# A decoder layer in float32: weight sums of the 7-product pieces of the down projection made by adding DMAs into a DRAM scratch, four pairs of k tiles per half instead of three

## Chip, cores and metric

One NeuronCore of a Trainium2 chip. The metric is the device time of one execution in microseconds (us), as the median of several. Engines are named as in the profile: PE (TensorE), DVE (VectorE), ACT (ScalarE), POOL (GpSimd), SP (SyncE, which here only issues DMAs).

## What is computed

A decoder layer on 256 tokens of width 2048. The change touches its last part, the feed-forward network:

```python
h = rmsnorm(x, g_pre_ffn[l])
up = causal_dwconv(h @ w_up[l], w_fconv[l], b_fconv[l])
gate, val = jnp.split(up, 2, axis=-1)
x = x + rmsnorm((jax.nn.gelu(gate, approximate=True) * val) @ w_down[l], g_post_ffn[l])
```

`w_up` is 2048 x 11264, `w_down` 5632 x 2048. Ahead of it stand, in this order, the input projections with latent attention (16 heads), the gates and the attention's output projection, a gated linear recurrence, the output projection, and a cross-attention; their result, the residual x3, goes into this part and is added at its end.

## The kernel before

**Pieces.** All weights stream through four slots of `raw` (128 partitions x 2048 columns, 1 MB a slot). Each piece is split into a high part (ACT, a rounding copy to float32r, `hi`, L1151) and a low part (DVE, raw minus high, `lo`, L1686), both in the same slot of `wsp`. PE multiplies with three terms: high x high, low x high, high x low (`TERMS`, `rows_mm`, L607; for whole feature tiles L544, where the first two are one matmul). SP issues the load of a piece when the low part of the piece four before it is done; ACT starts on a piece when PE has left the piece four before it; ACT and DVE run two pieces ahead of PE (`LEAD`). Each engine runs its instructions in the order of the code; ACT and DVE also evict tiles, and what is queued behind a waiting instruction waits too. Semaphores `landed`, `hi_done`, `lo_done` and `gemm_step` count these steps.

**The feed-forward stages.** The hidden features are made in three groups, of 16, 16 and 12 tiles of 128 (`GROUPS`). For each group 8 (or 6) up rounds (`up_round`) of four pieces make two hidden tiles each: ACT and DVE evict, scale, add the convolution and apply the gelu; POOL multiplies gate and value (L2550). Then the down stage multiplies the group's hidden tiles (the k tiles) with `w_down` and adds the result to the output.

**Seven products.** In the first two groups the down stage has two halves of 1024 output columns, 12 pieces each (`DN_PLAN`, `dn_half`). A pair of k tiles, the two blocks of 128 tokens and the two blocks of 512 columns make a 2 x 2 block product. A "plain" piece does it with 8 block products, 24 matmuls of 512 columns. Three of eight pairs do it in seven products (Strassen's scheme in Winograd's form). Such a pair has two pieces: "first" (9 matmuls), with weight blocks as they are, and "made" (12 matmuls), with sums and differences of weight blocks. DVE makes those sums from the "first" piece in the slot behind it (`sums_two`, `sums_rest`, L2303, L2309, L2310), so a "made" piece has no load. The last pair is two "single" pieces (12 matmuls each). The left-hand sums, the forms, come from two hidden tiles: POOL makes them (`form_sums`), ACT the high part (`form_high`, L1541), DVE the low part (`form_low`, L2218), in the up rounds.

**Where forms and x3 lie.** `forms` is laid over `big_a`, in which x3 stays for the residual. So x3 is stored in a DRAM tensor (`x3_kept`, in the trace `x_kept`) by a DMA of ACT behind up round 0 (L1585), and loaded back before the last group. ACT waits for the store behind its round 1:

```python
up_round(1)
if n == 0:
    act.wait_ge(x3_spilled, 16)
with act.Fori(1, up.trips // 2) as r:
    up_round(r * 2, formed=r - 1)
    up_round(r * 2 + 1)
```

**Between halves.** The product sums take four banks of PSUM, which the next half's plain pieces need. When the last "made" piece of a half is done ACT copies one bank (`q1_keep`, L1617) and DVE combines the others (`products_out`, L2332 to L2343); `plain_out` adds the plain banks.

**POOL** normalizes in attention (L2496), does elementwise work of the recurrence (L2509 to L2523) and of the up rounds, and issues no DMA.

## Time and profile before

| | us |
|---|---|
| median of 3 runs | 1728.7 (1728.68 to 1729.89) |
| the profiled execution | 1728.19 |
| its span | 1726.4 |
| PE busy | 1717.3 (99%) |
| DVE busy | 1210.6 (70%) |
| ACT busy | 943.0 (55%) |
| POOL busy | 168.9 (10%) |

The span runs from the first to the last instruction of the profiled execution. PE busy is the time in which a matmul was in flight. MB is 1024 x 1024 bytes where a transfer's size is told (the profile gives KB), and GB/s is the profile's own. The mean DMA rate over the span is 194 GB/s.

### The profile page before, as it was taken

The page shows a single profiled execution, that of the slowest core. Times are in us where ns is not written, and L with a number is a line of the kernel's source. Part 1 is how long each engine was busy: PE and PEld are TensorE (multiplying, and loading weights), DVE is VectorE, ACT ScalarE, POOL GpSimd, SP SyncE. Part 2 cuts the span into 40 slices and gives each one's busy share as a digit, 9 for nine tenths or more (in the row PEclk, how much of TensorE's full clock was granted, in tenths as well). Part 3 has the DMA queues.
Part 4 walks back from the last instruction along what each step waited for, and adds up shares of the span by engine and source line. Part 5 has one row for each costly group of instructions (what it writes and reads, how often), then busy time and mean ns, then how long its engine had stood idle before and what let it go on. Part 6 is the DMA issues. An engine that isn't in the chain of part 4 may idle for free.

```text
span 1726.4 us, 25016 instructions
## 1 busy us (share of the span) xinstructions
PE 1717.3 (99%) x8932; PEld 1463.5 (85%) x8932; DVE 1210.6 (70%) x1519; ACT 943.0 (55%) x1201; POOL 168.9 (10%) x201
## 2 busy tenths in 40 slices
PE   9999999999999999999999999999999999999998
PEld 8888888888888888888888888888888888888886
DVE  7766665467788874446567687778877778877766
ACT  7656655443667763334447565555555555445553
POOL 0012210000344520000000001110001110000000
PEclk9999999999999999999999999999999999999999
DMA  9644456565556565556655465554665554585552
GB/s 341 201 136 157 152 198 230 191 244 187 174 177 190 173 230 191 192 193 233 219 178 173 146 214 181 189 194 162 209 214 183 179 177 162 207 271 184 194 215 102
DMA packets 218719, 334.31 MB, mean 194 GB/s; under 512 B 5792, under 2 KB 162080, under 8 KB 215072
## 3 DMA queue, kind: packets, MB, share of 16 engines
q1 hardware_dynamic: 212736, 318.53, 55.1%
q10 hardware_dynamic: 5920, 14.94, 2.4%
q8 instruction: 40, 0.66, 0.2%
q14 instruction: 23, 0.19, 0.0%
HBM read 329.25 MB, written 4.19 MB: 193 GB/s over the span
## 4 chain that ended last, share of the span: by engine, by line
PE 98%; DVE 1%; DMA 0%; ACT 0%; issue 0%; DVEq 0%; SPq 0%
PE ps L544 51%; PE ps L607 36%; PE ps L1023 3%; PE ps L560 3%; PE ps L819 1%; PE ps L747 1%; PE ps L669 1%; PE ps L658 0%; PE ps L639 0%; PE ps L776 0%; PE ps L752 0%; PE ps L769 0%; DVE wsp L1686 0%; PE ps L663 0%; PE ps L777 0%; PE ps L907 0%
## 5 line engine op out<-in xcount | busy, mean ns | idle before, releaser
L1686 DVE TENSOR_TENSOR wsp<-raw,wsp 128x2048 fp32r<-128x2048 f32 (+3 forms) x307 | 673.1, 2209 | 256.5 <-ACT wsp L1151 249.6
L1151 ACT ACTIVATE wsp<-raw 128x2048 fp32r<-128x2048 f32 (+3 forms) x296 | 537.3, 1831 | 197.5 <-PE ps L607 182.9
L544 PE MATMUL ps<-asp,wsp 128*128 128x512 f32 x3064 | 542.4, 339 | 0.4 <-DVE wsp L1686 0.2
L544 PEld LDWEIGHTS ps<-asp,wsp 128*128 128x128 f32 x3064 | 469.6, 188 | 71.1 <-issue 1.4
L607 PE MATMUL ps<-wsp,hsp 128*128 128x512 f32 x2004 | 459.2, 390 | 0.2 <-DVE wsp L1686 0.2
L607 PEld LDWEIGHTS ps<-wsp,hsp 128*128 128x128 f32 x2004 | 375.7, 188 | 78.8 <-DVE wsp L1686 1.1
L544 PE MATMUL ps<-hsp,wsp 128*128 128x512 f32 (+1 forms) x1936 | 349.7, 340 | 0.0
L544 PEld LDWEIGHTS ps<-hsp,wsp 128*128 128x128 f32 x1936 | 297.5, 188 | 42.9
L607 PE MATMUL ps<-wsp,asp 128*128 128x512 f32 x768 | 175.6, 389 | 0.0
L1162 ACT ACTIVATE cr<-ps 128x256 f32<-128x256 f32 x185 | 69.3, 380 | 191.0 <-PE ps L544 171.9
L607 PEld LDWEIGHTS ps<-wsp,asp 128*128 128x128 f32 x768 | 143.9, 188 | 29.8
L2550 POOL TENSOR_TENSOR scr<-scr 128x256 f32<-128x256 f32 x44 | 34.2, 797 | 984.3 <-DVE scr L2246 984.3
L1551 ACT ACTIVATE scr<-scr,par 128x256 f32<-128x256 f32 x88 | 48.2, 596 | 63.4 <-DVE scr L2235 63.4
L2240 DVE SCALAR_TENSOR_TENSOR scr<-scr,par 128x255 f32<-128x255 f32 x88 | 42.5, 484 | 25.5 <-ACT scr L1551 25.2
L1694 DVE TENSOR_TENSOR cr<-ps,cr 128x256 f32<-128x256 f32 x88 | 35.1, 420 | 34.1 <-ACT cr L1162 34.1
L2518 POOL TENSOR_TENSOR scr<-scr 128x256 f32<-128x256 f32 x16 | 28.6, 1789 | 246.7 <-ACT scr L1342 246.7
L1579 ACT ACTIVATE hsp<-scr 128x256 f32 (+1 forms) x44 | 18.5, 420 | 53.1 <-POOL scr L2550 53.1
L560 PE MATMUL ps<-wsp,asp 128*128 128x512 f32 (+1 forms) x256 | 47.5, 341 | 0.0
L560 PEld LDWEIGHTS ps<-wsp,asp 128*128 128x128 f32 x256 | 40.0, 188 | 5.8
L2280 DVE TENSOR_TENSOR hsp<-scr,hsp 128x256 f32 (+1 forms) x44 | 19.8, 450 | 35.4 <-ACT hsp L1579 35.4
L1602 ACT ACTIVATE wsp<-raw 128x2048 fp32r<-128x2048 f32 x12 | 23.1, 1922 | 36.8 <-DVE raw L2310 25.0
L1261 ACT ACTIVATE scr<-scr,st 128x128 f32<-128x128 f32 (+1 forms) x32 | 14.4, 450 | 48.2 <-DVE st L1868 48.2
(291 smaller groups left out, 1191.8 us busy)
## 6 DMA issues: line engine op xcount, KB each, us to landing
raw<-in_w_up SPq DMA_DIRECT2D x88, 1024.0 KB, 5.3
raw<-in_w_in SPq DMA_DIRECT2D x64, 1024.0 KB, 5.4
raw<-in_w_down SPq DMA_DIRECT2D x40, 1024.0 KB, 5.0
raw<-in_w_in SPq DMA_DIRECT2D x32, 768.0 KB, 4.5
raw<-in_w_o_mla SPq DMA_DIRECT2D x16, 1024.0 KB, 5.2
raw<-in_w_o_lru SPq DMA_DIRECT2D x16, 1024.0 KB, 5.1
raw<-in_w_out SPq DMA_DIRECT2D x16, 1024.0 KB, 4.9
raw<-in_w_ukv SPq DMA_DIRECT2D x8, 1024.0 KB, 5.5
```

Of the source, the lines that this page charges most:

```text
L544: mm = pe.matmul(ps[:, bank, 0:w], lhs(part, k), x[:, 0:w], start=(f and part == 0), stop=(l and n == 1))
L560: mm = pe.matmul(o, x, r, start=(f and part == 0), stop=(l and n == 1))
L607: mm = pe.matmul(ps[:, bank, :], src[:, k, low * T + m * P:low * T + (m + 1) * P], wsp[:, c, part, cols], start=(first and t == 0), stop=( ...
L1023: mm = pe.matmul(ps[:, bank, :], lhs(low), wsp[:, slot, part, quarter(block)], start=(first and t == 0), stop=(last and t == 2))
L1151: act.activation(wsp[:, p0 % SLOTS, 0, 0:n], raw[:, p0 % SLOTS, 0:n], ACT.Copy).then_inc(hi_done, 1)
L1162: act.activation(cr[:, slot, :], ps[:, bank, T:2 * T], ACT.Copy, scale=scale).then_inc(cross_done, 1)
L1551: act.activation(UC[2 * v + e], UR[2 * v + e], ACT.Identity, scale=col(W_F + 2 * P, m), bias=col(B_F, m)).then_inc(up_bias, 1)
L1686: dve.tensor_tensor(wsp[:, slot, 1, 0:n], raw[:, slot, 0:n], wsp[:, slot, 0, 0:n].bitcast(F32), ALU.subtract).then_inc(lo_done, 1)
L1694: return dve.tensor_tensor(dst, ps[:, bank, 0:T], cr[:, slot, :], ALU.add)
L2240: own.mark(dve.scalar_tensor_tensor(out=buf[:, 1:T], in0=src[:, 0:T - 1], scalar=col(W_F + P, m), in1=buf[:, 1:T], op0=ALU.mult, op1=ALU.add))
L2518: own.mark(pool.tensor_tensor(IG[e], IG[e], XC[e], ALU.mult))
L2550: pool.tensor_tensor(HID[e], UC[e], UC[2 + e], ALU.mult).then_inc(hid_out, 1)
```

## The change

**Plan.** Each half now has four product pairs (0, 2, 4, 6) and four plain ones (1, 3, 5, 7); the "single" pieces are gone. The last piece of a half is a plain pair.

**Weight sums.** For each "made" piece (8 a group) POOL builds the 128 x 2048 block in the DRAM tensor `dn_sums`: two copies of 128 x 512 from `w_down`, two DMAs that add to them, then twice a copy inside the scratch and an adding DMA. It does so for batches of 3, 3 and 2 pieces and waits after each of six steps of a batch. The first group's sums stand in POOL's order between attention and the recurrence, the second group's between the recurrence and the up rounds. SP loads a "made" piece from the scratch; a "first" piece is loaded in two DMAs, without its first block of 512 columns, which its matmuls don't use. The additions on DVE are gone.

**Forms.** Each group has four forms instead of three, written in the odd up rounds 1, 3, 5, 7 instead of 2, 4, 6. ACT's wait for the store of x3 moves in front of round 1.

**Order.** `q1_keep` and `products_out` stand one piece later in ACT's and DVE's order (behind piece 12 of a stage, where the last "made" piece is number 10; before, behind piece 11 with the last "made" piece number 9).

```diff
-DN_PLAN = [("plain", 0), ("plain", 2), ("plain", 4), ("plain", 6), ("first", 1), ("made", 1),
-           ("first", 3), ("made", 3), ("first", 5), ("made", 5), ("single", 14), ("single", 15),
...
+DN_HALF = [("plain", 1), ("plain", 3), ("first", 0), ("made", 0), ("first", 2), ("made", 2),
+           ("plain", 5), ("first", 4), ("made", 4), ("first", 6), ("made", 6), ("plain", 7)]
+DN_PLAN = DN_HALF + DN_HALF
...
+DN_SUMS = [DN_MADE[0:3], DN_MADE[3:6], DN_MADE[6:8]]
...
# SP
+                        sp.wait_ge(lo_done, dn.p(0, c) - SLOTS + 1)
+                        if kind == "first":
+                            sp.dma_start(raw[:, slot, 512:1024], w_dn[:, k, c0 + 512:c0 + 1024]).then_inc(landed[slot], 16)
+                            sp.dma_start(raw[:, slot, 1024:2048], w_dn[:, k + 1, c0:c0 + 1024]).then_inc(landed[slot], 16)
+                        else:
+                            at = DN_MADE.index(c) + len(DN_MADE) * n
+                            sp.wait_ge(dn_sums_step, sums_ready(n, c))
+                            sp.dma_start(raw[:, slot, :], dn_sums[at]).then_inc(landed[slot], 16)
...
# ACT
                     if n == 0:
                         act.wait_ge(x3_sq, 2)
                         act.dma_start(x3_kept, a_tok).then_inc(x3_spilled, 16)
-                    up_round(1)
-                    if n == 0:
                         act.wait_ge(x3_spilled, 16)
+                    up_round(1, formed=0)
                     with act.Fori(1, up.trips // 2) as r:
-                        up_round(r * 2, formed=r - 1)
-                        up_round(r * 2 + 1)
+                        up_round(r * 2)
+                        up_round(r * 2 + 1, formed=r)
...
# DVE
                     for c in range(LEAD, 24 + LEAD):
-                        if c + 1 in DN_FIRST:
-                            sums_two(c + 1)
...
-                        if c + 1 in DN_FIRST:
-                            sums_rest(c + 1)
-                        if c in (11, 23):
-                            products_out(c // 12)
+                        if c in (12, 24):
+                            products_out(c // 24)
...
# POOL
+            def weight_sums(n, cs, done):
...
+                def step(count):
+                    done[0] += 16 * count * len(cs)
+                    pool.wait_ge(dn_sums_step, done[0])
+                for at in cs:
+                    for e in range(2):
+                        pool.dma_start(to(at, e), block(at, 0, 0)).then_inc(dn_sums_step, 16)
+                step(2)
+                for at in cs:
+                    pool.dma_start(to(at, 0), block(at, 0, 1), accum_op=ALU.add).then_inc(dn_sums_step, 16)
+                    pool.dma_start(to(at, 1), block(at, 1, 0), accum_op=ALU.add).then_inc(dn_sums_step, 16)
+                step(2)
+                for frm, into, k, b in ((0, 2, 1, 0), (2, 3, 1, 1)):
+                    for at in cs:
+                        pool.dma_start(to(at, into), to(at, frm)).then_inc(dn_sums_step, 16)
+                    step(1)
+                    for at in cs:
+                        pool.dma_start(to(at, into), block(at, k, b), accum_op=ALU.add).then_inc(dn_sums_step, 16)
+                    step(1)
```

**In ACT's order**, behind up round 0 of the first group (`wsp<-raw` is the high part of a piece, `cr<-ps` an eviction, `hsp<-scr` the hidden tiles' high part, `x_kept` the store's target). Before:

```order
L1579 ACTIVATE hsp<-scr 128x256 [waits hid_out] x2
L1585 DMA x_kept<-big_a 128x4096 [waits x3_sq]
L1151 ACTIVATE wsp<-raw 128x2048 [waits landed2,gemm_step]
L1151 ACTIVATE wsp<-raw 128x2048 [waits landed3,gemm_step]
L1162 ACTIVATE cr<-ps 128x256 [waits up_ready,tile_out,gemm_step] x2
```

Now:

```order
L1590 ACTIVATE hsp<-scr 128x256 [waits hid_out] x2
L1596 DMA x_kept<-big_a 128x4096 [waits x3_sq]
L1162 ACTIVATE wsp<-raw 128x2048 [waits landed2,gemm_step,x3_spilled]
L1552 ACTIVATE forms<-scr 128x4x128 [waits fm_raw]
L1162 ACTIVATE wsp<-raw 128x2048 [waits landed3,gemm_step]
L1173 ACTIVATE cr<-ps 128x256 [waits up_ready,tile_out,gemm_step] x2
```

The wait on `x3_spilled` has come to the first high part behind the store, and a form stands between the two high parts.

**In DVE's order**, around the end of the first half of group 0 (`scr<-cols_in,ps` and the next three are `products_out`). Before:

```order
L1686 TENSOR_TENSOR wsp<-raw,wsp 128x1024 [waits hi_done] x2
L2332 TENSOR_TENSOR scr<-cols_in,ps 128x512 [waits q1_out,gemm_step]
L2340 TENSOR_TENSOR cols_in<-scr,ps 128x512 [waits dn_out]
L2341 TENSOR_TENSOR cols_in<-ps,scr 128x512
L2343 TENSOR_TENSOR cols_in<-ps,cols_in 128x512 [waits dn_out]
L1686 TENSOR_TENSOR wsp<-raw,wsp 128x2048 [waits hi_done] x2
```

Now:

```order
L2300 TENSOR_TENSOR wsp<-raw,wsp 128x1536 [waits hi_done]
L1687 TENSOR_TENSOR wsp<-raw,wsp 128x2048 [waits hi_done] x3
L2316 TENSOR_TENSOR scr<-cols_in,ps 128x512 [waits q1_out,gemm_step]
L2324 TENSOR_TENSOR cols_in<-scr,ps 128x512 [waits dn_out]
L2325 TENSOR_TENSOR cols_in<-ps,scr 128x512
L2327 TENSOR_TENSOR cols_in<-ps,cols_in 128x512 [waits dn_out]
L1687 TENSOR_TENSOR wsp<-raw,wsp 128x2048 [waits hi_done]
```

Behind the last "made" piece two low parts stand ahead of `products_out` now (pieces 11 and 12), where both of the "single" pieces stood, and one instead of two follows before the next half's first product piece.

## Rows read from the trace of the kernel before

**Rows 1.** The page: busy time of each engine, and the granted clock by slice.

```profile
span 1726.4 us, 25016 instructions
...
PE 1717.3 (99%) x8932; PEld 1463.5 (85%) x8932; DVE 1210.6 (70%) x1519; ACT 943.0 (55%) x1201; POOL 168.9 (10%) x201
...
PEclk9999999999999999999999999999999999999999
```

**Rows 2.** Waits of PE, whole span: who was waited for, us, times, longest.

```profile
PE ps L1128 <- ACT mask L1666: 2.2, 1, 2.2
...
PE ps L544 <- DVE wsp L1686: 0.2, 1, 0.2
...
PE ps L607 <- DVE wsp L1686: 0.2, 1, 0.2
```

**Rows 3.** The chain of waits: start us, us, what.

```profile
271.48 114.29 PE ps L607 x504
...
1007.33 163.20 PE ps L544 x928
...
1192.30 14.29 PE ps L1023 x63
```

**Rows 4.** The chain, at the end of group 0's first half.

```profile
1206.61 0.61 ACT cols_in L1617
...
1207.32 0.70 DVE scr L2332
...
1209.93 2.21 DVE wsp L1686
```

**Rows 5.** Timeline of DVE, down stage: start us, us, instruction, count, idle before.

```profile
1180.56 1.22 DVE L2303 TENSOR_TENSOR raw<-raw 128x1024 f32<-128x1024 f32 x1
...
1184.62 0.69 DVE L2310 TENSOR_TENSOR raw<-raw 128x512 f32<-128x512 f32 x1
```

**Rows 6.** Tile forms: ns min/median/max of one form's high part, and when.

```profile
L1541 ACT ACTIVATE forms<-scr x6: 615/616/637, 1042.5 to 1397.3; 128x512 f32 x6
```

**Rows 7.** Windows: stretch, busy of PE, PEld, DVE, ACT, POOL, clock, DMA share, GB/s.

```profile
263.00:443.00 180.00, 180.00 (x824) 150.03 (x823) 104.78 (x107) 81.80 (x65) 0.56 (x1) 1.00 0.62 212
0.00:35.00 35.00, 33.41 (x150) 27.66 (x151) 25.84 (x51) 25.71 (x40) 1.78 (x11) 1.00 0.98 348
```

**Rows 8.** Timeline of ACT around the store of x3.

```profile
1018.80 0.35 ACTq L1585 DMA_DIRECT2D x_kept<-big_a  x1
1019.25 3.73 ACT L1151 ACTIVATE wsp<-raw 128x2048 fp32r<-128x2048 f32 x2
```

**Rows 9.** DMA issues by line, whole span: KB each, us to landing.

```profile
x_kept<-big_a ACTq DMA_DIRECT2D x1, 2048.0 KB, 6.5
```

**Rows 10.** Timeline of DVE, up round 1: the low parts of its pieces.

```profile
1021.20 4.49 DVE L1686 TENSOR_TENSOR wsp<-raw,wsp 128x2048 fp32r<-128x2048 f32 x2 [1.53 <-ACT wsp L1151]
```

**Rows 11.** End of the span: timeline of PE, then windows as in rows 7.

```profile
1721.32 0.67 PE L1128 MATMUL ps<-scr,mask 128*128 128x256 f32 x2 [2.19 <-ACT mask L1666]
...
1719.00:1721.00 2.00, 0.13 (x1) 0.00 (x0) 1.57 (x8) 1.03 (x4) 0.00 (x0) 1.00 0.00 0
...
1723.00:1724.00 1.00, 0.00 (x0) 0.00 (x0) 0.25 (x1) 0.00 (x0) 0.00 (x0) 0.67 1.03 354
1724.00:1725.00 1.00, 0.00 (x0) 0.00 (x0) 0.00 (x0) 0.00 (x0) 0.00 (x0) 0.50 1.05 366
```

**Rows 12.** Timeline of POOL: end of attention, the recurrence, the first up round.

```profile
443.05 0.74 POOL L2518 TENSOR_TENSOR scr<-scr 128x256 f32<-128x256 f32 x1 [179.48 <-ACT scr L1342]
446.76 0.74 POOL L2521 TENSOR_TENSOR scr<-scr 128x256 f32<-128x256 f32 x1 [2.98 <-ACT scr L1349]
...
1017.21 1.55 POOL L2550 TENSOR_TENSOR scr<-scr 128x256 f32<-128x256 f32 x2 [390.11 <-DVE scr L2246]
```

**Rows 13.** DMA issues by line: the weights of this stage and the output.

```profile
raw<-in_w_o_mla SPq DMA_DIRECT2D x16, 1024.0 KB, 5.2
...
out<-raw SPq DMA_DIRECT2D x7, 256.0 KB, 2.5
```

More of the change, by code:

```diff
@@ L77, with sums_ready, __init__ @@
 W_F, B_F = 256, 640
+DN_SUMS = [DN_MADE[0:3], DN_MADE[3:6], DN_MADE[6:8]]
+def sums_ready(n, c):
+    turn = [c in cs for cs in DN_SUMS].index(True)
+    return 16 * 8 * (n * len(DN_MADE) + sum(len(cs) for cs in DN_SUMS[:turn + 1]))
 class Phase:
-    def __init__(self, after, trips, ends, crosses=True, made=()):
+    def __init__(self, after, trips, ends, crosses=True, twice=()):
         self.trips, self.ends, self.n = trips, ends, len(ends)
@@ L101, in __init__ @@
         self.x_end = self.x0 + (self.tiles * trips if crosses else 0)
-        self.made = (after.made if after else []) + [self.p0 + c for c in made]
-        assert self.n % SLOTS == 0 and (not made or trips == 1)
+        self.twice = (after.twice if after else []) + [self.p0 + c for c in twice]
+        assert self.n % SLOTS == 0 and (not twice or trips == 1)
     def p(self, i, c):
@@ L118, in landed @@
         at = self.p0 + c
-        skipped = sum(q < at and q % SLOTS == at % SLOTS for q in self.made)
-        return i * (16 * self.n // SLOTS) + 16 * (at // SLOTS + 1 - skipped)
+        more = sum(q <= at and q % SLOTS == at % SLOTS for q in self.twice)
+        return i * (16 * self.n // SLOTS) + 16 * (at // SLOTS + 1 + more)
 class Tally:
@@ L161 @@
     if _count % 16 == 0:
-        PH_DN.append(Phase(PH_UP[-1], 1, [0] * 24, made=DN_MADE))
+        PH_DN.append(Phase(PH_UP[-1], 1, [0] * 24, twice=DN_FIRST))
     else:
@@ L357, in piece_size @@
         def piece_size(ph, i, c):
-            if ph.n == len(DN_PLAN) and c < ph.n and DN_PLAN[c][0] == "single":
-                return 1024
             if ph is PH_A:
@@ L1043, in dn_half @@
                         (kind, pair), slot = DN_PLAN[c], c % SLOTS
-                        k0, k1 = (pair, pair) if kind == "single" else (2 * pair, 2 * pair + 1)
+                        k0, k1 = 2 * pair, 2 * pair + 1
                         arrive(dn, 0, c)
@@ L1060, in dn_half @@
                                         mm = x_mm(c, k, m, b, first=(k == k0))
+                        elif c == mine[-1]:
+                            for m in range(2):
+                                for b in range(2):
+                                    for k in (k0, k1):
+                                        mm = x_mm(c, k, m, b, last=(k == k1))
+                                    if (m, b) != (1, 1):
+                                        mm.then_inc(dn_done, 1)
                         elif kind == "plain":
@@ L2500, in _, with to, block @@
                 attention(u)
+            def weight_sums(n, cs, done):
+                def to(at, first, count=1):
+                    return dn_sums[len(DN_MADE) * n + DN_MADE.index(at)][:, first * 512:(first + count) * 512]
+                def block(at, k, b):
+                    k, c0 = GROUPS[n][0] + 2 * DN_PLAN[at][1] + k, (at // 12) * 1024 + b * 512
+                    return w_dn[:, k, c0:c0 + 512]
+                def step(count):
[16 more added lines that the diff above has]
+                    step(1)
+            sums_done = [0]
+            for cs in DN_SUMS:
+                weight_sums(0, cs, sums_done)
             n0 = own.n
@@ L2552, in up_pair @@
                 def up_pair(r):
-                    own.n, own.off = n0 + 6 * n, r * 2
+                    own.n, own.off = n0 + 8 * n, r * 2
                     up_round(r * 2)
+                    form_sums(n, r)
                     up_round(r * 2 + 1)
-                    form_sums(n, r)
                 if fn == 16:
                     up_pair(0)
-                    with pool.Fori(1, up.trips // 2 - 1) as r:
+                    with pool.Fori(1, up.trips // 2) as r:
                         up_pair(r)
-                    for i in range(up.trips - 2, up.trips):
-                        up_round(i)
                 else:
```

73 lines of the change are left out of this document (23 added, 50 removed).

## Prediction

> **What bounds the kernel now.** I read the page first: TensorE (PE) is busy for 1717.3 of 1726.4 us at full granted clock [rows 1]. Then the waits of PE: the longest is 2.2 us, at the end, and only two of 0.2 us are for work that the change touches [rows 2]. So the time is the number of matmuls times their pace, and a change gains only by removing matmuls; every microsecond in which PE must wait is added. The chain of waits says the same and gives the pace: 504 matmuls of 512 columns take 114.29 us, 63 in the product pieces 14.29 us, 0.2268 us each [rows 3]. VectorE (DVE) and ScalarE (ACT) are under 75% busy [rows 1], so relief for them is worth nothing by itself.
>
> **The matmuls.** A pair of k tiles costs 24 matmuls as a plain piece (2 k, 2 row blocks, 2 column blocks, 3 terms) and 21 as products (9 in a "first" piece, 12 in a "made" one). A half had 3 pairs as products and 5 plain (the last cut into two "single" pieces): 63 + 120 = 183. It now has 4 and 4: 84 + 96 = 180. Three matmuls fewer in each of 4 halves (2 groups of 16 tiles, 2 halves): 12 x 0.2268 = **2.7 us less**, all on the bounding engine.
>
> **The hand-over between halves.** Before, the plain pieces of half 1 (and the first up piece behind half 1) waited a little for a DVE subtraction of 2.21 us that stood behind the four additions of the product sums [rows 4]: two waits of PE of 0.2 us [rows 2]. Now that subtraction stands ahead of these additions. Its input needs PE to be through with piece 8, and 9 + 12 matmuls (4.8 us) follow before the last "made" piece ends, so it is done by then; the additions take 0.61 + 4 x 0.7 = 3.3 us beside a plain piece of 5.4 us. Worth **0.4 us less**.
>
> **Additions taken off DVE.** Of each "made" piece 1.22 + 0.69 + 0.69 us of DVE work go [rows 5], 12 times, 31 us. PE waited for none of it [rows 2], so this counts nothing. The added fourth form per group costs ACT 0.62 us [rows 6], and DVE about as much for 512 columns [rows 5], between pieces as the other three; nothing.
>
> **The loads of the down stage.** "made" pieces had no load; now each has one of 1 MB, and "first" has 0.75 MB instead of 1. A half needs 4 x 1 + 4 x 1.75 = 11 MB in 180 x 0.2268 = 40.8 us. Full DMA share moved about 348 GB/s [rows 7], 3.0 us per MB, so 33 of 40.8 us. A buffer is free when its subtraction is done, which is more than a piece ahead of its use; following pieces one by one with 2 us from issue to the first byte and 3.1 us per MB, the tightest piece lands 5.6 us before it is needed. No term, but little is left for anything slower.
>
> **The spill of x3, moved wait.** This is the term that decides. Forms lie over the buffer that holds x3, so x3 must be stored in DRAM before the first form is written. The first form is now made in up round 1, not round 2, so ACT's wait for the store has moved from behind round 1 to directly behind its issue. ACT issued the store at 1018.80 [rows 8]; it needs 6.5 us to landing [rows 9], so ACT stands until 1025.3. What is queued behind it is the high part of round 1's third piece, which began at 1019.25 [rows 8]. Its low part on DVE began 1.95 us after that and takes 2.25 us (4.49 for two) [rows 10]: now ready at 1025.3 + 1.95 + 2.25 = 1029.5. PE wants the piece three pieces after 1007.33; 928 matmuls (29 pieces) take 163.20 us, 5.63 a piece [rows 3], so at 1024.2. Before, it was ready at 1023.45, only 0.8 us early. So PE stands still for **5.3 us**, once. The form (0.62 us on ACT) goes between this piece and the next, which is then ready near 1032.4 against 1035.1 wanted, and the pieces of round 2 some 1.5 us early: no second stall. Nothing gives this back, since PE never waits there otherwise. In the second group the wait doesn't exist.
>
> **The clock behind that stall.** No row has a gap of 5 us inside the work. At the end PE was idle for 2.19 us before 1721.32 at granted clock 1.00; after its last matmul, which ended at 1721.99, the clock was 0.67 in 1723 to 1724 and 0.50 from 1724 on [rows 11], that is half speed within 2 us of idleness. A stall of 5.3 us may well end at 1.2 GHz. What half speed then costs is between nothing (it comes back at once) and a piece's 5.6 us (one piece at half speed); no row shows a return, so I take the middle, **2.8 us more**. The Trainium skill (TensorE: Matmul & The Clock Gate, Part 1) says that the throttled clock is the default and only activity releases it, which speaks against this change: a stall is paid a second time after it ends. By it the sum has this term, by the 2.2 us gap that passed at full clock it has not; the end of the trace agrees with the rule as to the fall, and no run here yet shows the return.
>
> **The sum.** 1728.2 (the profiled execution; span 1726.4 and 1.8 around it) - 2.7 - 0.4 + 5.3 + 2.8 = 1733.2; the median shown is 0.5 above the profiled one, so **1733.7 us**.
>
> **Is the scratch made in time?** GpSimd (POOL) now issues 64 DMAs of 256 KB for each group, in 18 steps with a wait after each. The first group's stand between attention's last multiply, ended 179.48 us before 443.05, at 263.6, and the first multiply of the recurrence at 443.05; the next really waited-for one is at 446.76 [rows 12], so there are 183 us. No row has a DMA issued by POOL, a DRAM to DRAM copy or an add. Nearest rows: 2 MB in 6.5 us [rows 9] and 256 KB in 2.5 us [rows 13], so 1.9 us fixed and 2.3 us per MB. With an add counted as twice its bytes, a batch of 3 takes 5.4 + 8.8 + 3.6 + 5.4 + 3.6 + 5.4 = 32 us, that of 2 takes 25: **90 us alone**, 35 of them fixed and 55 transfer. Beside it the weight loads have a DMA share of 0.62 [rows 7]. If both queues take turns the transfers double: 145 us. If the loads go first, 55 / 0.38 + 35 = 180 us. I take 145, since two queues with work are likelier to alternate; cost nothing, cover 38 us. The second group has the 390 us before 1017.21 [rows 12]. The weight loads themselves may be slowed by this: a load is issued when the piece in its buffer is split, some 4 us after PE gave back the buffers that this split writes, and it is wanted when they come free again, four pieces of 5.4 us later. So it may take some 17 us, against 5.2 now [rows 13].
>
> **Rivals.**
> 1. *The clock stays up.* As above without the 2.8: 1731.0 us, a loss of 0.13% that a measurement can't tell. For it: the 2.2 us gap. Against: the fall within 2 us at the end [rows 11]. 15%.
> 2. *The scratch is late.* POOL's queue is in order, so attention's successor, the recurrence, waits behind the DMAs; its scan on DVE and with it the splitting of weights wait, and PE within some 5 us. It decides if an add costs more than three times a plain transfer: with four, (18 + 73) x 2 + 35 = 217 us, 34 us late, 1768 us. Making descriptors on POOL could do the same. For it: a chain of 18 waits, and a window that fits by 38 us only by assumption. Against: nearest rows give 90 to 180. 22%.
> 3. *The other side: no stall.* The stored x3 lands by 1020.0 (1024.2 less the 4.2 us of splitting), or ACT's wait isn't at the queue's head. Then only the saved matmuls show: 1725.6 us, 0.18% less, not slower. It decides at a landing of 1.2 us, which a 2 MB store can't reach at any rate in the rows; left is that I misread who needs the piece. 8%.
> 4. *Loads starve* in the down stage or beside the adds, by some pieces of a few us: about 1738. 5%.
>
> **How the numbers follow.** A measurement of this kernel tells 0.2%, 3.5 us, from no change. My forecast, stall and clock, has 50%; its own range is 1731 to 1736.6 (clock cost 0 to 5.6), nearly all of it slower by over 0.2%: 0.43. With rivals 2 and 4 slower is 0.69. Same: 0.07 of the forecast, rival 1, most of rival 3, 0.28. Faster 0.03. The range starts at 1730, leaving out rival 3, and ends at 1757, leaving out the worse half of rival 2.
>
> **What would show it.** PE's matmul count 8920 instead of 8932; one wait of PE of about 5 us near 1024, on DVE's low part behind ACT, with ACT idle until the store lands; granted clock under 1.00 right after; no PE wait near the halves; POOL's last DMA of the first group landed before the recurrence's multiply. Wrong would be a recurrence that starts late, PE waits on loads, or no gap near the first up rounds.

## The result, and the profile after

| | before | after |
|---|---|---|
| median | 1728.7 | 1799.29 (1798.07 to 1806.63, 5 runs) |
| the profiled execution | 1728.19 | 1806.63 |
| its span | 1726.4 | 1804.5 |

The changed kernel takes 1.0422 times as long (95% interval 1.0405 to 1.0439). The forecast was 1733.7 with a range up to 1757. Two of the five executions took 1806.4 and 1806.6 us, three 1798.1 to 1799.3; the trace is of one of the longer, and no trace shows where the others are 7 us shorter. The page of the changed kernel, busy times and granted clock:

```profile
span 1804.5 us, 25148 instructions
PE 1718.7 (95%) x8920; PEld 1465.3 (81%) x8920; DVE 1191.2 (66%) x1485; ACT 950.1 (53%) x1203; POOL 259.2 (14%) x335
...
PEclk9999999999659999999999999999999999999999
```

Beside [rows 1]: PE's busy time is the same within 1.4 us, the matmuls are 12 fewer, and the span is 78 us longer. So the time is in waits. PE's waits, in the same view as [rows 2]:

```profile
PE ps L554 <- DVE wsp L1687: 76.8, 2, 71.5
PE ps L1139 <- ACT mask L1667: 2.2, 1, 2.2
...
PE ps L665 <- ACT wsp L1199: 0.6, 1, 0.6
```

The first line holds two waits: 76.8 - 71.5 = 5.3 us is the stall behind the store of x3, to the tenth what the prediction's steps give. The other, 71.5 us, was rival 2's. The 0.6 us lie 10 us into the kernel; the trace of the kernel before has no such wait there, and of the experiments' traces, in which that part of the code is the same, some have it and some have not. PE's timeline has both stalls (start us, us, instruction, count, idle before):

```profile
532.09 7.58 PE L554 MATMUL ps<-hsp,wsp 128*128 128x512 f32 x32 [71.49 <-DVE wsp L1687]
...
1103.72 8.63 PE L554 MATMUL ps<-asp,wsp 128*128 128x512 f32 x33 [5.30 <-DVE wsp L1687]
```

At the first, the profile names DVE's low part as what PE waited for. Following the waits back one engine at a time: DVE's low part stands in its order behind the recurrence's scan, the scan waits for POOL's multiply, and POOL was not computing at all. The waits of DVE and of ACT over the whole span, of each the longest line on POOL:

```profile
DVE scr L1980 <- POOL scr L2533: 82.5, 9, 73.4
...
ACT asp L1335 <- POOL scr L2519: 74.8, 4, 68.3
```

The timeline of POOL, from attention's last multiply to the first one of the recurrence:

```profile
264.32 3.36 POOL L2496 DMA_DIRECT2D dn_sums<-in_w_down  x6
277.29 0.90 POOL L2499 DMA_DIRECT2D dn_sums<-in_w_down  x1 [9.60 <-DMA dn_sums<-in_w_down]
287.57 0.83 POOL L2500 DMA_DIRECT2D dn_sums<-in_w_down  x1 [9.38 <-issue]
...
298.32 0.81 POOL L2500 DMA_DIRECT2D dn_sums<-in_w_down  x1 [9.08 <-issue]
...
471.13 0.56 POOL L2496 DMA_DIRECT2D dn_sums<-in_w_down  x1 [8.54 <-DMA dn_sums<-in_w_down]
...
518.59 0.82 POOL L2507 DMA_DIRECT2D dn_sums<-in_w_down  x1 [3.77 <-issue]
523.04 0.72 POOL L2528 TENSOR_TENSOR scr<-scr 128x256 f32<-128x256 f32 x1 [3.62 <-DMA dn_sums<-in_w_down]
```

The first group's sums take 264.3 to 523.0, 259 us, where the prediction had 145 and 183 us of room. Two kinds of waits alternate: for the landing of a step's DMAs ("<-DMA", the program's own wait), and in front of a DMA in the middle of a step ("<-issue", a wait for nothing that the profile shows). The second kind was in no step of the prediction. The recurrence started at 523.0 instead of 443 [rows 12].

The half clock behind the stalls shows in windows, columns as in [rows 7]:

```profile
534.00:536.00 2.00, 2.00 (x9) 1.74 (x8) 2.00 (x6) 0.89 (x1) 0.00 (x0) 0.55 1.05 371
536.00:538.00 2.00, 2.00 (x14) 1.72 (x13) 2.00 (x7) 0.00 (x0) 0.00 (x0) 1.00 1.09 354
...
1102.00:1103.00 1.00, 0.00 (x0) 0.00 (x0) 1.00 (x1) 1.00 (x1) 0.00 (x0) 0.71 0.00 0
1103.00:1105.00 2.00, 1.28 (x4) 1.10 (x5) 2.00 (x3) 1.12 (x3) 0.00 (x0) 0.50 0.07 13
1105.00:1107.00 2.00, 2.00 (x8) 1.71 (x7) 2.00 (x4) 0.00 (x0) 0.00 (x0) 0.50 0.94 308
1107.00:1109.00 2.00, 2.00 (x9) 1.71 (x7) 1.66 (x6) 1.58 (x3) 0.00 (x0) 0.50 1.07 357
1109.00:1110.00 1.00, 1.00 (x6) 0.91 (x6) 0.82 (x3) 1.00 (x1) 0.00 (x0) 0.88 1.09 358
```

A window of 2 us at half speed counts 8 or 9 matmuls, one at full speed 14. Behind the short stall, work runs at half speed from 1103.7 to about 1109.2 (0.88 is 0.24 us at half speed), 5.5 us, half of which is lost: 2.8 us. Behind the long one it is 532.1 to 535.8, 3.7 us, so 1.9 us lost. The whole difference then adds up for the profiled execution (the hand-over is sized in the part on the prediction):

1728.2 - 2.7 (matmuls) - 1.4 (hand-over) + 5.3 (stall at the store) + 2.8 (its half clock) + 71.5 (recurrence late) + 1.9 (its half clock) + 0.6 (the wait at 10 us) = 1806.2, against 1806.63 measured.

What remained open was why the sums took 259 us. In the stretch of [rows 7] the DMA share went from 0.62 to 0.91:

```profile
263.00:443.00 180.00, 180.00 (x825) 150.01 (x824) 105.21 (x108) 82.02 (x65) 29.78 (x45) 1.00 0.91 270
```

and the weight loads there went from 5.2 us to landing [rows 13] to 10.1. In these rows of the DMA issues, the copies and adds of 256 KB take 5.6 and 7.1 us, where the prediction took 2.5 (the row of a 256 KB output store) with the transfer doubled:

```profile
dn_sums<-in_w_down POOLq DMA_DIRECT2D x96, 256.0 KB, 7.1
raw<-in_w_o_mla SPq DMA_DIRECT2D x16, 1024.0 KB, 10.1
...
dn_sums<-dn_sums POOLq DMA_DIRECT2D x32, 256.0 KB, 5.6
```

### The profile page after: what moved, and what is told of

It is laid out like the page before. It is cut to its first block, busy times and chain, and to the rows that moved or that the text cites. A ratio compares the mean times of both kernels' runs of the same rounds, so it can differ in the third digit from the quotient of the medians.

```text
span 1804.5 us, 25148 instructions
## 1 busy us (share of the span) xinstructions
PE 1718.7 (95%) x8920; PEld 1465.3 (81%) x8920; DVE 1191.2 (66%) x1485; ACT 950.1 (53%) x1203; POOL 259.2 (14%) x335
## 3 DMA queue, kind: packets, MB, share of 16 engines
q0 software_dynamic: 14336, 33.56, 10.2%
## 4 chain that ended last, share of the span: by engine, by line
PE 82%; DMA 8%; issue 7%; POOL 2%; DVE 1%; ACT 0%; SPq 0%; DVEq 0%; POOLq 0%
PE ps L554 46%; PE ps L617 24%; DMA dn_sums<-in_w_down 5%; PE ps L1033 4%; PE ps L570 2%; DMA dn_sums<-dn_sums 2%; PE ps L829 1%; PE ps L679 1%; PE ps L757 1%; POOL dn_sums L2507 0%; POOL dn_sums L2496 0%; PE ps L649 0%; DVE wsp L1687 0%; DMA x_kept<-big_a 0%; DMA raw<-in_w_in 0%
## 5 line engine op out<-in xcount | busy, mean ns | idle before, releaser
L1687 DVE TENSOR_TENSOR wsp<-raw,wsp 128x2048 fp32r<-128x2048 f32 (+2 forms) x303 | 673.4, 2236 | 284.9 <-ACT wsp L1162 281.6
L1162 ACT ACTIVATE wsp<-raw 128x2048 fp32r<-128x2048 f32 (+2 forms) x304 | 560.2, 1856 | 238.3 <-PE ps L617 191.3
L617 PE MATMUL ps<-wsp,hsp 128*128 128x512 f32 x1908 | 437.2, 390 | 0.0
L554 PE MATMUL ps<-hsp,wsp 128*128 128x512 f32 (+1 forms) x1936 | 351.6, 341 | 71.5 <-DVE wsp L1687 71.5
L617 PEld LDWEIGHTS ps<-wsp,hsp 128*128 128x128 f32 x1908 | 357.9, 188 | 74.1
L2563 POOL TENSOR_TENSOR scr<-scr 128x256 f32<-128x256 f32 x44 | 34.3, 798 | 705.6 <-DVE scr L2247 705.6
L1980 DVE TENSOR_TENSOR_SCAN scr<-scr 128x256 f32<-128x256 f32 x16 | 19.7, 1230 | 82.5 <-POOL scr L2533 82.5
L2507 POOL DMA_DIRECT2D dn_sums<-in_w_down x32 | 27.0, 966 | 133.5 <-DMA dn_sums<-dn_sums 77.5
L1033 PE MATMUL ps<-wsp,forms 128*128 128x512 f32 x192 | 46.1, 389 | 0.0
L1335 ACT ACTIVATE asp<-scr 128x256 f32 (+1 forms) x16 | 6.0, 412 | 74.8 <-POOL scr L2519 74.8
## 6 DMA issues: line engine op xcount, KB each, us to landing
raw<-in_w_o_mla SPq DMA_DIRECT2D x16, 1024.0 KB, 10.1
```

The source lines that it names most:

```text
L554: mm = pe.matmul(ps[:, bank, 0:w], lhs(part, k), x[:, 0:w], start=(f and part == 0), stop=(l and n == 1))
L617: mm = pe.matmul(ps[:, bank, :], src[:, k, low * T + m * P:low * T + (m + 1) * P], wsp[:, c, part, cols], start=(first and t == 0), stop=( ...
L1033: mm = pe.matmul(ps[:, bank, :], lhs(low), wsp[:, slot, part, quarter(block)], start=(first and t == 0), stop=(last and t == 2))
L1162: act.activation(wsp[:, p0 % SLOTS, 0, 0:n], raw[:, p0 % SLOTS, 0:n], ACT.Copy).then_inc(hi_done, 1)
L1687: dve.tensor_tensor(wsp[:, slot, 1, 0:n], raw[:, slot, 0:n], wsp[:, slot, 0, 0:n].bitcast(F32), ALU.subtract).then_inc(lo_done, 1)
L2507: pool.dma_start(to(at, into), block(at, k, b), accum_op=ALU.add).then_inc(dn_sums_step, 16)
```

## The experiments

The expectations name causes by letters; those of the first two are explained in their own words, the others are these. **C**: the chain, 18 steps each with a full landing, whatever is in them. **W**: the sums get only what the weight loads leave of the DMA engines. The first two experiments are for the part that the prediction had sized.

**1. No sums at all.** SP loads the "made" piece from `w_down` (one block of 1 MB), POOL issues nothing:

```diff
-                            sp.wait_ge(dn_sums_step, sums_ready(n, c))
-                            sp.dma_start(raw[:, slot, :], dn_sums[at]).then_inc(landed[slot], 16)
+                            sp.dma_start(raw[:, slot, :].rearrange("p (k c) -> p k c", k=2), w_dn[:, k:k + 2, c0:c0 + 1024]).then_inc(landed[slot], 16)
...
-            for cs in DN_SUMS:
-                weight_sums(0, cs, sums_done)
...
-            for cs in DN_SUMS:
-                weight_sums(1, cs, sums_done)
```

> The changed kernel without any DMA of POOL; a made piece is loaded from the down weights themselves (same size, so the output of the down stage is not the reference's). Theory L (lateness of the scratch is the whole of the miss): the stall of 71.5 us and 2.0 us of half clock behind it go, all else stays: 1728.7 - 2.7 - 0.4 + 5.3 + 2.7 = 1733.6 us, about 5 us above before, with one PE wait of 5.3 us in the first up rounds. Rival B (the rest also carries cost: loads of the down stage, contention later on): more than 1736.

Measured: 1732.15 us (1730.91 to 1733.53, 11 runs), ratio to the kernel before 1.0019 (1.0010 to 1.0028). The waits of PE:

```profile
PE ps L553 <- DVE wsp L1686: 5.2, 1, 5.2
```

The 71.5 us are gone, the 5.2 us are left, and the time is 1.5 us under its expectation. So everything beyond about 4 us belongs to POOL's DMAs, and the forecast of 1733.7 was a forecast of this kernel.

**2. The same, and the wait for the store one piece later.** ACT makes both high parts of round 1's next pieces first, then waits for x3's store and makes the form; DVE's low half of the form moves behind its low parts in the same way:

```diff
+                        if stored:
+                            act.wait_ge(x3_spilled, 16)
+                            form_high(n, formed)
...
-                        act.wait_ge(x3_spilled, 16)
-                    up_round(1, formed=0)
+                    up_round(1, formed=0, stored=(n == 0))
```

> As the first run (no DMA of POOL, made pieces from the down weights), but in the first group's up round 1 ACT splits both of its next pieces before it waits for the store of x3, and the form comes behind them (on DVE too). Theory S (the moved wait costs a 5.3 us stall and 2.7 us of half clock): both go, 1725.6 us, 8 us less than the first run and 3.1 less than before. Rival: the stall moves to the pieces of round 2, and less than 4 of the 8 us come back.

Measured: 1724.33 us (1724.19 to 1725.08, 10 runs), ratio 0.9976 (0.9967 to 0.9986), 7.8 us less than experiment 1. ACT's timeline there:

```profile
1019.03 3.72 ACT L1161 ACTIVATE wsp<-raw 128x2048 fp32r<-128x2048 f32 x2
1025.03 0.63 ACT L1551 ACTIVATE forms<-scr 128x512 fp32r<-128x512 f32 x1 [2.27 <-DMA x_kept<-big_a]
```

The store still lands no earlier, but only 2.27 us of it are waited for, and nobody waits for the form. So the stall cost its own 5.2 us and 2.6 us more. In the trace of experiment 1 the clock comes back at 1034.3, after 3.9 us of work at half speed, so 1.9 us of the 2.6 are the clock's; 0.6 us are the wait at 10 us, which experiment 1's trace has and this one has not.

**3. Twice the room for descriptors:** `dynamic_dma_scratch_size=2048` instead of 1024, nothing else.

> The changed kernel with dynamic_dma_scratch_size 2048 instead of 1024, nothing else. Theory R (POOL stands at an issue because there is no room for the descriptors of the next DMA; some 100 us of the first group's 258): these waits shrink to a few, the sums of the first group take 180 to 210 us (their transfers, 95 us at full share, still compete with the loads), time 1735 to 1765. Theory A (the adds themselves are slow) and theory C (the chain of 18 waits): the room changes nothing, 1795 to 1805.

Measured: 1772.93 us (1771.75 to 1774.3, 4 runs), ratio 1.0256 (1.0240 to 1.0271); the sums 225 us. The "<-issue" waits fell from 90.5 to 49.5 us, so these are waits for room. R is a cause, but neither the only one nor as large as its expectation had it. The sums are 34 us shorter and the profiled execution 33 us; between the medians it is 26 us, since the change's trace is of a longer execution.

**4. The adds as copies** (`accum_op=ALU.add` removed), room 1024 again. Of the 8 DMAs of a piece 4 add, 32 of a group's 64.

```diff
-                    pool.dma_start(to(at, 0), block(at, 0, 1), accum_op=ALU.add).then_inc(dn_sums_step, 16)
+                    pool.dma_start(to(at, 0), block(at, 0, 1)).then_inc(dn_sums_step, 16)
...
-                        pool.dma_start(to(at, into), block(at, k, b), accum_op=ALU.add).then_inc(dn_sums_step, 16)
+                        pool.dma_start(to(at, into), block(at, k, b)).then_inc(dn_sums_step, 16)
```

> The changed kernel with every adding DMA of POOL replaced by a plain copy of the same block (the scratch then holds no sums, so the down stage's output is not the reference's); same number of DMAs, steps and waits, room 1024. Theory A (an add costs 2.8 times a copy in the DMA engines): the share of POOL's queue falls from 95 to some 50 us for the first group, its sums take about 150 us, in time, 1733 to 1740. Theory C (18 waits in series): they take over 220 us, 1765 or more. Theory R: the same as C unless an add also needs more descriptors than a copy; then no waits at issue are left either.

Measured: 1748.68 us (1747.54 to 1749.81, 2 runs), ratio 1.0116 (1.0097 to 1.0134); the sums 201 us, between the expectations of A (150) and C (over 220). So the adds cost 58 us, for 32 of them. How, the queue's rows tell (packets, MB, share of 16 engines). In the changed kernel:

```profile
q0 software_dynamic: 14336, 33.56, 10.2%
```

And with copies:

```profile
q0 software_dynamic: 10240, 33.56, 7.4%
```

The 128 copying DMAs of the two groups are 80 packets each; with 64 of them adding there are 4096 more, 64 for each add, 144 against 80. The same MB are listed. 10.2% of 1804.5 are 184 us of the 16 engines, 7.4% of 1745.6 are 129: the difference over 64 is 0.86 us an add, on top of 1.0 us for a copy, 1.9 times in all. That is the factor of two that the prediction allowed, and less than the 2.8 of A's expectation. But more packets fill the room sooner, and POOL needs longer to issue one. From POOL's timeline with copies:

```profile
275.79 0.52 POOL L2499 DMA_DIRECT2D dn_sums<-in_w_down  x1 [8.51 <-DMA dn_sums<-in_w_down]
283.61 0.54 POOL L2500 DMA_DIRECT2D dn_sums<-in_w_down  x1 [7.30 <-issue]
...
304.93 0.53 POOL L2504 DMA_DIRECT2D dn_sums<-dn_sums  x1 [7.52 <-issue]
```

**5. One batch instead of three** (6 steps of 8 or 16 DMAs for 18 steps of 2 to 6), room 2048. It is compared with experiment 3.

```diff
-DN_SUMS = [DN_MADE[0:3], DN_MADE[3:6], DN_MADE[6:8]]
+DN_SUMS = [DN_MADE[0:8]]
```

> The changed kernel with room for descriptors of 2048 (as e3_scratch_2048) and all 8 pieces of a group in one batch: 6 waits for a group instead of 18, same DMAs and bytes. Theory C (the chain of waits, each with its latency to landing, sets the 225 us that the sums took in e3): 12 waits of some 6 us fewer, the first group's sums take 150 to 165 us, in time, 1731 to 1734 us. Theory W (the loads go first and the sums have what they leave of the DMA engines: 86 us of engine time / 0.38 = 226): still 215 to 235 us, 1763 to 1783.

Measured: 1743.07 us (1741.10 to 1745.04, 2 runs), ratio 1.0082 (1.0064 to 1.0101); the sums 198 us, between the two expectations. Waits for landing fell from 131 to 61 us, as C wants, but those for room rose from 49.5 to 93.2: a longer step only meets the room instead. And now the loads suffer. The waits of PE:

```profile
PE ps L554 <- DVE wsp L1687: 9.6, 2, 5.3
PE ps L617 <- DVE wsp L1687: 4.4, 1, 4.4
```

The window of the same kernel, columns as in [rows 7]:

```profile
263.00:443.00 180.00, 175.63 (x790) 145.47 (x789) 99.74 (x98) 78.90 (x61) 39.71 (x60) 0.99 1.01 290
```

The second line's wait, at 303.6, lies in the projections beside the sums, where the engines are full (share 1.01). The loads beside the first group's sums took 15.0 and 16.2 us (medians by line), and the prediction had said that some 17 is what one may take. The five issued from 266.8 to 293.2, just ahead of the wait, took more:

```profile
L397 SPq DMA_DIRECT2D raw<-in_w_in x5: 368/368/1549, 266.8 to 293.2; - x5
...
DMA to landing us min/median/max: 16.1/21.7/23.8
```

The one of 23.8 us was issued at 275.4 and landed at 299.2; ACT's high part and DVE's low part follow it at once and end at 303.6, where PE goes on.

**6. Half the weight loads** beside the sums (512 KB a piece in the gates' and the attention output's projections), room 1024, adds as in the change.

```diff
+                if ph is PH_GM or ph is PH_OM:
+                    piece(ph, i, c, 2, 512, w[:, 4 * (c % 4):4 * (c % 4) + 2, bass.ds(col, 512)])
+                    return
```

> The changed kernel (room 1024, batches of 3, 3, 2), but in the two token stages beside the sums each weight load brings only half of its piece; the other half of the buffer holds old data, so the output is not the reference's. Theory W: the loads' share of the engines falls from 0.62 to about 0.33, the sums take 95 / 0.67 = 140 to 160 us, in time, 1731 to 1735. Theory C: the 18 waits and the waits for room stay, each a little shorter, over 200 us, 1750 or more.

Measured: 1795.33 us (1795.19 to 1795.47, 2 runs), ratio 1.0384 (1.0365 to 1.0403); the sums 249 us, 10 less; the median is 4.0 us less, which is no more than the change's own executions lie apart. W falls: the DMA share of the window is 0.83 instead of 0.91, and the sums hardly noticed.

```profile
263.00:443.00 180.00, 180.00 (x824) 150.01 (x823) 104.86 (x107) 81.87 (x65) 31.15 (x46) 1.00 0.83 205
```

The trace of the change itself goes further. With PE stalled the loads stopped too: SP's last packet before the gap ended at 457.0 and its next began at 533.2. So the third batch, from 471.1 to 523.0, had the DMA engines to itself. From the DMA view of 466 to 523, in which no other queue appears:

```profile
q0 software_dynamic: 1973, 4.51, 47.9%
...
dn_sums<-in_w_down POOLq DMA_DIRECT2D x12, 256.0 KB, 4.8
dn_sums<-dn_sums POOLq DMA_DIRECT2D x4, 256.0 KB, 4.0
```

This batch of 2 pieces took 51.9 us (28 waiting for landings, 13 for room, 11 issuing), and the prediction's price for it, alone, was 25. Scaled to all eight pieces, the chain alone would take 156 us by its steps (18 for 6) or 208 by its DMAs (64 for 16), an estimate. So the price of 90 us alone was too low by 66 to 118 us before any neighbour is counted.

**7. Copies and room 2048 together** (experiments 3 and 4 in one). Here A is the theory that the two costs simply add up, S (here and in 8) the chain of steps, L (in 8) that the loads set what is left.

> The change with both of the earlier single edits: the descriptor room is 2048 instead of 1024, and the 40 adding DMAs of a group copy instead (the pieces then hold copied blocks instead of sums, so the output isn't the reference's; DMA count, bytes of the 18 steps and all else stay). Sums of the first group took 258 us with neither edit, 225 with the room alone, 201 with the copies alone. Theory S (a serial chain: each of 18 steps is the issue of its DMAs, 1.6 to 3.1 us, and then one landing of about 7 us beside the loads, whatever the DMAs do; room and adds cost on top only where the room runs out): without adds few descriptors are needed, so most of what the room gives is already in the copies' 57 us; waits of POOL for issue (40 us with the copies alone) fall to under 5 us, and part of that comes back as longer waits for landings; the sums take 175 to 190 us, time 1731 to 1740. Theory A (the two costs are independent and add up): 258 - 33 - 57 = 168 us or less, under the 183 us of room, no wait of PE beyond the 5.3 us of the store of x3: 1731 to 1734. If the loads alone set the pace nothing changes: 198 to 201 us, 1748.

Measured: 1738.02 us (1737.97 to 1739.27, 3 runs), ratio 1.0059 (1.0036 to 1.0082); the sums 192 us. The room saves 34 us with adds and 9 with copies. Turned round, the adds cost 58 us with the small room, of which 50 are waits for room (the table below), and still 33 with the large one. (Its expectation counts 40 adding DMAs a group where there are 32; its numbers don't use that count.) The additive theory (168 us) falls; the chain's 175 to 190 was missed by 2 us. What is left are landings, one after the other. The waits of POOL from 263 to 524:

```profile
POOL dn_sums L2504 <- DMA dn_sums<-in_w_down: 54.0, 6, 13.7
POOL dn_sums L2507 <- DMA dn_sums<-dn_sums: 43.4, 6, 9.0
...
POOL dn_sums L2496 <- issue: 7.8, 1, 7.8
POOL dn_sums L2504 <- issue: 7.6, 1, 7.6
```

Six waits for landing at each of L2504 and L2507 alone, 97 of 192 us, for steps of two to six transfers of 256 KB.

**8. The same with half the loads.**

> As the kernel with copies instead of adds and room of 2048, and beside it the weight loads of the gates' and the attention output's projections move half of each piece (512 KB instead of 1 MB; the other half of a slot keeps what it held, so the output isn't the reference's for this reason too). Theory S: what is left is 18 times issue and one landing; a landing of 256 KB beside half the loads is perhaps 6 instead of 7 us, so 18 x (2 + 6) = 145 to 165 us, never near the 90 us that the prediction gave for the sums alone. Theory L (once the adds and the room are out of the way the loads' traffic sets the rest, as the prediction had it): the transfers take 55 us plus a turn for each load, under 125 us. Time by both about 1731 to 1734, as only the stall behind the store of x3 is left.

Measured: 1731.96 us (1730.78 to 1732.66, 8 runs), ratio 1.0020 (1.0009 to 1.0031). The last DMA was issued at 431.1, and those of its line take 6.1 to 7.8 us, so the sums took 173 to 175 us, above the 145 to 165 of the chain and far above the 125 of the prediction's own picture (transfers and turns, L). PE's only new wait is the 5.3 us at the store.

**What each edit does to the 259 us.** From POOL's waits in the first group (the rest is the time of its 64 issuing instructions). The row of the change is of an execution 7 us above its median, so a small difference from it, the 10 us of half the loads above all, tells little:

| kernel | sums, us | waits for landing | waits for room | issuing |
|---|---|---|---|---|
| the change | 259 | 124 | 90 | 44 |
| room 2048 | 225 | 131 | 50 | 45 |
| copies | 201 | 127 | 40 | 34 |
| copies, room 2048 | 192 | 143 | 15 | 34 |
| half the loads | 249 | 116 | 89 | 44 |
| one batch, room 2048 | 198 | 61 | 93 | 44 |

And the stall of PE follows from the first column: in the change, experiments 3, 4, 6 and 7 the sums end at 523.0, 489.2, 464.7, 512.6 and 455.4, and PE's stall is 71.5, 37.6, 13.4, 61.9 and 4.6 us. The difference is 451 every time, within half a us. (In experiment 5 PE was 6 us behind already, by its wait at 303.6 and the half clock after it, and its stall is 4.3 us for sums that end at 461.7.) So there were 187 us, 4 more than the prediction's 183, and each us beyond them is a us of the kernel.

**9. A version that keeps both edits harmless.** All sums as in the change, room 2048, the wait for the store as in experiment 2, and the third batch of the first group moved in POOL's order behind the recurrence, where the second group's sums stand and POOL has 390 us [rows 12]:

```diff
-            for cs in DN_SUMS:
+            for cs in DN_SUMS[:2]:
                 weight_sums(0, cs, sums_done)
...
+            for cs in DN_SUMS[2:]:
+                weight_sums(0, cs, sums_done)
```

> Room 2048, the late wait of e2_no_sums_spill_late, and the first group's third batch moved behind the recurrence, ahead of the second group's. In e3 two batches took 264.3 to 444.8, and the recurrence needs POOL at 446.8: just in time. Behind it 44 + 236 = 280 us in a gap of 390. If the lateness is all, 1724.3 as without sums, up to 1727 if the second batch ends late by some us. Slower than 1730 would mean that the sums cost something else too.

Measured: 1724.87 us (1724.29 to 1725.77, 11 runs), ratio 0.9977 (0.9968 to 0.9986). The sums behind the recurrence ran from 628 to about 935, before POOL's first product of the up rounds at 1017 [rows 12]. It is as expected, but tight: the recurrence's first multiply on POOL began at 447.23, straight behind a wait for a DMA, 4 us before it would have cost.

**10. The same with 5 pieces before and 3 behind** (batches of 3, 2 and 3).

> As e7_two_batches_before, with batches of 3, 2 and 3, of which the first two (5 pieces) stand before the recurrence. They end some 30 us before POOL is needed (5/6 of 180 us): 1724.3 as without sums, and no PE wait in the recurrence. 3 pieces of the first group and 8 of the second behind it: 11/8 of 236 = 325 us in 390. Rival: the loads of the stages beside the sums come late somewhere, 1727 or more.

Measured: 1724.76 us (1724.28 to 1726.13, 10 runs), ratio 0.9977 (0.9968 to 0.9987). POOL's timeline, from its last DMA before the recurrence:

```profile
415.90 1.73 POOL L2511 DMA_DIRECT2D dn_sums<-in_w_down  x2 [6.88 <-DMA dn_sums<-dn_sums]
443.73 0.73 POOL L2532 TENSOR_TENSOR scr<-scr 128x256 f32<-128x256 f32 x1 [26.10 <-ACT scr L1353]
```

All waits of PE:

```profile
PE ps L1139 <- ACT mask L1669: 2.2, 1, 2.2
PE ps L643 <- POOL ident L2459: 1.5, 1, 1.5
PE ps L971 <- DVE big_a L2158: 0.2, 1, 0.2
```

POOL now waits 26 us for ACT instead of being waited for, and no wait of PE is new. This version beats both kernels: 4.0 us (0.23%) under the kernel before. Its time is that of experiment 2, which had no sums, within 0.4 us, so sums that are early cost nothing that can be measured here.

## Why the prediction was wrong, step by step

**The matmuls, -2.7: right.** The count is 8920.

**The hand-over, -0.4: right in kind, too small.** Experiment 2 holds these two terms alone and lies 4.3 us under before, for 3.1. The rest is at the halves. PE's timeline at the end of group 0's down stage, before:

```profile
1248.36 5.60 PE L607 MATMUL ps<-wsp,hsp 128*128 128x512 f32 x24
1254.20 8.12 PE L544 MATMUL ps<-asp,wsp 128*128 128x512 f32 x45 [0.24 <-DVE wsp L1686]
```

And in experiment 2:

```profile
1246.34 5.60 PE L616 MATMUL ps<-wsp,hsp 128*128 128x512 f32 x24
1251.78 10.60 PE L553 MATMUL ps<-asp,wsp 128*128 128x512 f32 x59
```

From the first matmul of the piece to what follows it are 5.84 us before and 5.44 now. Before, all four ends of a half had such a delay: 0.44, 0.41, 0.31 and 0.28 us beyond the usual 0.227 from one matmul's start to the next, 1.4 us together. The view of the waits lists two of them, with 0.2 us each, since it counts from a matmul's end, 0.39 us after its start. Now there is none, in the changed kernel either. The two down stages take 4.2 us less together, 2.7 by matmuls and 1.4 by this, which is nearly all of the 4.3. (The prediction's 3.3 us of additions are 3.4 by its own terms; nothing hangs on it.)

**Loads of the down stage, 0: right.** No wait of PE lies there, neither in the changed kernel nor in experiments 1 and 2.

**The store of x3, +5.3: right**, 5.3 and 5.2 measured. The landing took 6.3 us (6.5 taken), ACT stood idle for 5.90 us, and the low part on DVE was the one that PE waited for:

```profile
1093.04 0.35 ACTq L1596 DMA_DIRECT2D x_kept<-big_a  x1
1099.35 1.91 ACT L1162 ACTIVATE wsp<-raw 128x2048 fp32r<-128x2048 f32 x1 [5.90 <-DMA x_kept<-big_a]
```

**The clock, +2.8: right in kind, and in size by luck.** It was a midpoint between 0 and 5.6. In the change's trace the clock fell 4.0 us after the last matmul (at 1098.4), in the window 1102 to 1103 (0.71), and held half speed for 5.5 us of work after the stall, 2.8 us lost. In the eight traces that have this same stall of 5.2 to 5.3 us the work at half speed lasts from 3.0 us (experiment 6) to 6.1 (experiments 3 and 7), so 1.5 to 3.0 us are lost. The Trainium skill (TensorE: Matmul & The Clock Gate, Part 1), weighed in the prediction, says that activity must release the clock again; the windows agree, with those 5.5 us. Rival 1 (the clock stays up) falls.

**"Is the scratch made in time?" failed, and with it the forecast.** The sentence was "I take 145, since two queues with work are likelier to alternate; cost nothing, cover 38 us". The measured time is 259 us. The step failed before any neighbour is counted: the price alone, 90 us for the chain and 25 for its last batch, held only the bytes and 1.9 us a step, and that batch took 51.9 us alone (experiment 6). Its parts against the measured ones:
- *Issuing counted as nothing.* 64 DMAs occupy POOL for 44 us: 0.52 us for a copy, 0.81 and more for an add. The prediction gave each step one fixed time, however many DMAs it issues.
- *Waits for room counted as nothing*: 90 us, the largest miss. Rival 2 had them in half a sentence ("making descriptors on POOL could do the same") without a price or a range. Experiments 3, 4 and 7 show them: 90, 50, 40 and 15 us with less need or more room.
- *Landings*: 124 us (143 when nothing else holds POOL up) against 145. So the number that was argued at length came out about right, but by luck: its two halves, 35 us fixed and 110 of transfer, were both off. The nearest rows gave 1.9 us fixed and 0.6 us for 256 KB; measured was 5.6 to 7.1 us to landing, 4.0 to 4.8 with nothing beside it, and half the loads took only 1.1 us off (7.3 in experiment 7, 6.2 in experiment 8).
- *Which queue yields* did not decide. The prediction's three bounds, 90, 145 and 180, varied only this; experiment 6 took half the loads away and found 10 us. All three bounds came from one uncertainty, and the two others had none.

**Rival 2's mechanism was the one that happened**, order and engines included: the recurrence behind POOL's DMAs, the scan, the splitting, PE. Its size and its point of decision were off: it was to need an add of more than three plain transfers, and an add is 1.9 times a copy on the DMA engines. It gave 34 us late and 1768 us; it was 71.5 us late in the traced execution, and the median is 1799.3 us.

**The second group, 0: right.** Its sums ran from 701 to about 985, even longer (284 us), inside POOL's 390 us of idleness.

**Rival 3 (no stall at the store)** falls: the stall is there in every kernel whose ACT waits in front of the first high part, and gone where it doesn't (experiments 2, 9 and 10).

**Rival 4 (loads starve)** did not occur in the change, where a load beside the sums took 10 to 11 us (15.8 at most) of the 17 allowed, but did in experiment 5 (4.4 us, behind a load of 23.8 us). Loads of up to 19.0 us passed there without a wait, so that bound held roughly.

## What to carry to other kernels

A chain of small DMAs with a wait after each step is priced by its steps, (issuing + one whole landing) each, and not by its bytes; on POOL add the descriptors' room, for which an in-order engine stands still. Put such a chain where its engine has twice the time that the sum gives, since what is queued behind it (here the recurrence) pays every microsecond of overrun. And when a term is kept at nothing by a cover, each quantity in it needs its own bound: three bounds of the same unknown look like a range and are not one.

## What the runs showed of the hardware

- **Waits for room come at a fixed count.** In the kernel with copies and room 1024, POOL stood in front of its 8th, 15th, 29th, 36th, 50th and 64th DMA of a group's 64: every seventh, where those missing (22nd, 43rd, 57th) are the first of a step, with everything landed anyway. With room 2048 it was the 15th and the 29th, every fourteenth (43rd and 57th are firsts of a step). Each lasted 3.5 to 9.7 us, about the landing of the DMA just ahead. The queue was emptied rather than fed as room came free: at the end of each of these waits of the first group every packet that POOL had issued had ended, the last one 0.7 to 1.8 us earlier. With adds they come sooner: in the first adding step of the change before its second and its fourth DMA (9.38 and 9.08 us).
- **A DMA that adds** in DRAM showed 144 packets against 80 for a copy of the same 256 KB, 1.9 us of the 16 engines against 1.0, and kept POOL for 0.81 us and more against 0.52.
- **Small transfers:** a DMA of 256 KB issued by POOL took 5.5 to 7.9 us to landing beside the full loads in steps of two to six (medians by line, first group's sums), 7.7 and 11.0 in experiment 5's steps of eight and sixteen, and 4.0 to 4.8 with nothing beside it; a single copy with nothing beside it took 3.6 us, a single add 4.4. The 256 KB output store of [rows 13], at the end of the span without weight loads, takes 2.5. The Trainium skill (DMA: Bandwidth & Descriptors, Anatomy of one DMA) gives 2.0 us and the bytes over 436 GB/s for a DMA issued by GpSimd, which is 2.6 us by estimate. For a copy from DRAM to DRAM the measured 3.6 us decide. By the formula the whole chain would be 75 us (18 x 2.0 + 64 x 0.6), also an estimate, less still than the prediction's 90 alone.
- **Loads pay for neighbours:** 1 MB loads went from 5.2 to 10.1 us beside the sums, and the DMA share from 0.62 to 0.91, without a wait of PE; at a share of 1.01, medians of 15.0 and 16.2 us and one load of 23.8, one came.
- **How long the half clock lasts does not go with the stall, and varies from run to run.** The traces have 15 stalls of PE inside the work, of 4.3 to 71.5 us. The clock fell 2.2 to 4.9 us after the last matmul, and the first 3.0 to 6.1 us of work behind the stall ran at 1.2 GHz: 3.7 us behind 71.5, 5.5 behind 5.3 in the same trace, and behind the 5.3 us of the store 3.0 in one run and 6.1 in another. At the end of the kernel before it fell 1.3 us after the last matmul (0.67 in the window 1723 to 1724, [rows 11]). The prediction read "half speed within 2 us of idleness" from that one place.
